# Products for the norms' sums on VectorE, a group later, and another order for the conversion of weight pieces round norms and woven groups

## What is computed

```python
for l in range(DEPTH):
    h = rmsnorm(x, norm_mix_pre[l])
    proj = h @ w_in[l]
    ...                       # three branches, gated and merged
    x = x + rmsnorm(merged @ w_o[l], norm_mix_post[l])
    h = rmsnorm(x, norm_ffn_pre[l])
    up = causal_dwconv(h @ w_up[l], ffn_conv_w[l])
    gate, val = jnp.split(up, 2, axis=-1)
    f = (jax.nn.silu(gate) * val) @ w_down[l]
    x = x + rmsnorm(f, norm_ffn_post[l])
```

## Time and profile before

| | |
|---|---|
| median of 3 runs | 1929.98 us (1924.31 to 1937.8) |
| the profiled execution | 1930.59 us |
| its span | 1928.9 us |
| TensorE busy | 1866.5 us, 97% |
| VectorE busy | 1375.6 us, 71% |
| ScalarE busy | 1083.3 us, 56% |
| GpSimd busy | 274.2 us, 14% |
| mean granted clock of TensorE | 0.986 |

### The profile page before, as it was taken

The page is one execution under the profiler, slowest core; times in us unless marked ns, Lnnn a source line. Parts: engine busy times, 40 slices in busy tenths (PEclk is TensorE's granted clock), DMA queues, the critical chain, the costliest instruction groups (busy, mean ns, idle before and its releaser), DMA issues.

```text
span 1928.9 us, 37388 instructions
## 1 busy us (share of the span) xinstructions
PE 1866.5 (97%) x15052; PEld 1818.9 (94%) x15052; DVE 1375.6 (71%) x2448; ACT 1083.3 (56%) x1820; POOL 274.2 (14%) x274
## 2 busy tenths in 40 slices
PE   7999989999999989999999999999998999999998
PEld 7999989999999989999889988999998999899998
DVE  5997678856888768876766777655557677776553
ACT  5455556654455556654666575545456757755442
POOL 1112420001103420002212103000012121030000
PEclk9999989999999989999999999999999999999999
DMA  7545535554545535564444433566544443345553
GB/s 262 170 158 187 165 121 194 182 193 142 182 159 180 167 114 199 188 207 143 153 140 137 132 131 122 177 195 195 191 161 137 148 143 117 117 164 170 192 196 111
DMA packets 86284, 315.45 MB, mean 164 GB/s; under 512 B 9568, under 2 KB 9952, under 8 KB 85984
## 3 DMA queue, kind: packets, MB, share of 16 engines
q1 hardware_dynamic: 86112, 313.06, 48.5%
HBM read 311.98 MB, written 1.05 MB: 162 GB/s over the span
## 4 chain that ended last, share of the span: by engine, by line
PE 83%; DVE 7%; ACT 6%; issue 2%; POOL 1%; DMA 0%; SPq 0%; DVEq 0%; ACTq 0%; POOLq 0%
PE big L568 73%; PE small L568 7%; ACT H L1825 3%; PE small L567 2%; DVE POOL L1305 1%; DVE L L1105 1%; DVE POOL L1189 1%; POOL POOL L2416 1%; PE small L571 0%; DVE X L1212 0%; DVE POOL L1204 0%; DVE gates L1322 0%; DVE POOL L1621 0%; DVE POOL L1434 0%; DVE POOL L1386 0%
## 5 line engine op out<-in xcount | busy, mean ns | idle before, releaser
L568 PE MATMUL big<-HH,H 128*128 128x256 f32 x3392 | 969.1, 286 | 16.8 <-DVE gates L1322 5.3
L568 PE MATMUL big<-HL,H 128*128 128x256 f32 x3392 | 948.8, 280 | 3.8 <-DVE HL L1236 3.8
L568 PE MATMUL big<-HH,L 128*128 128x256 f32 x3392 | 947.6, 279 | 0.0
L1825 ACT ACTIVATE H<-F 128x1024 fp32r<-128x1024 f32 x588 | 618.5, 1057 | 485.9 <-PE big L568 483.7
L1105 DVE TENSOR_TENSOR L<-F,H 128x1024 fp32r<-128x1024 f32 x584 | 714.7, 1232 | 197.1 <-ACT H L1825 196.6
L568 PEld LDWEIGHTS big<-HH,H 128*128 128x128 f32 x3392 | 645.0, 190 | 22.3 <-DVE gates L1322 6.0
L568 PEld LDWEIGHTS big<-HL,H 128*128 128x128 f32 x3392 | 643.1, 190 | 7.8 <-DVE HL L1236 5.2
L568 PEld LDWEIGHTS big<-HH,L 128*128 128x128 f32 x3392 | 643.3, 190 | 0.0
L568 PE MATMUL big<-FH,H 128*128 128x256 f32 x848 | 240.6, 284 | 0.1
L568 PE MATMUL big<-FL,H 128*128 128x256 f32 x848 | 236.7, 279 | 0.2
L568 PE MATMUL big<-FH,L 128*128 128x256 f32 x848 | 236.1, 278 | 0.0
(11 more groups left out here) (232 smaller groups left out, 1917.1 us busy)
## 6 DMA issues: line engine op xcount, KB each, us to landing
F<-in_stream SPq DMA_DIRECT2D x588, 512.0 KB, 3.4
X<-in_x SPq DMA_DIRECT2D x2, 512.0 KB, 4.3
out_x<-X SPq DMA_DIRECT2D x1, 1024.0 KB, 3.9
CO<-in_consts SPq DMA_DIRECT2D x1, 771.0 KB, 10.5
POOL<-in_decay SPq DMA_DIRECT2D x1, 768.0 KB, 11.8
PR<-in_params SPq DMA_DIRECT2D x1, 405.0 KB, 7.3
CO<-in_turn SPq DMA_DIRECT2D x1, 256.0 KB, 3.5
POOL<-in_lam SPq DMA_DIRECT2D x2, 128.0 KB, 3.8
```

Source lines behind the costliest of these rows:

```text
L568: return pe.e.matmul(out_, lhsT, rhs, start=start, stop=stop)
L1825: a.activation(H[:, j % NR, :], F[:, j % NF, :], ACT.Copy).then_inc(s_hi, 1)
```

## The change

1. The products x z (`xz`) of all eight j are made by VectorE in `summed`, behind the `yield`, that is in the loop turn of the next group, directly ahead of the add. The add waits for VectorE's own product instead of GpSimd's. GpSimd's `summed` is gone.
2. In ScalarE's norm the table preload stands ahead of the `HH` tiles, and for b > 0 a piece is converted behind tile 2 and another behind tile 4. Behind a group of full banks ScalarE evacuates first and converts then; the pieces of that group that begin after its middle are no longer converted in its own turn.
3. VectorE has one piece more to convert in halves ahead of and in a norm (`owed`), and two more halves in norms 1 to 4: ahead of the last normed tile and behind the last `HL` tile. Behind a group of full banks one piece is converted ahead of the evacuation of each member (`settle` with `low`).

TensorE's and SyncE's instructions stand in the same order as before.

```diff
@@ TensorE, sums_of @@
-                if j == 7:
-                    pe.wait_ge(bnd_v.sem, bnd_v.at(b, "xz"))
-                elif j:
-                    pe.wait_ge(bnd_g.sem, bnd_g.at(b, "xz", j))
+                if j:
+                    pe.wait_ge(bnd_v.sem, bnd_v.at(b, "xz", j))
@@ VectorE, norm @@
                 for n in range(KT):
+                    if n == KT - 1:
+                        low_half()
...
                     if n % 2:
                         low_x(layer, e, n - 1)
+                        if n == KT - 1:
+                            low_half()
@@ VectorE, summed @@
                 yield
-                if j == 7 and b in SUMMED:
+                if b in SUMMED:
+                    if j > 3:
+                        dve.wait_ge(bnd_v.sem, bnd_v.at(b, "add", j - 3))
                     dve.wait_ge(s_eva, m.act)
-                    v.tensor_tensor(squares_at(7, 2), X[:, j, :], tile(Z + j), ALU.mult).then_inc(
-                        bnd_v.sem, bnd_v.up(b, "xz"))
+                    v.tensor_tensor(squares_at(j, 2), X[:, j, :], tile(Z + j), ALU.mult).then_inc(
+                        bnd_v.sem, bnd_v.up(b, "xz", j))
...
-                    dve.wait_ge(bnd_g.sem, bnd_g.at(b, "xz", j))
+                    dve.wait_ge(bnd_v.sem, bnd_v.at(b, "xz", j))
@@ VectorE, settle and the main loop @@
-            def settle(n):
+            def settle(n, low=0):
                 for m in G[n].members:
+                    if low:
+                        low_parts(low)
+                        low += 1
...
                 if not made_after and full_banks(n - 1):
-                    settle(n - 1)
+                    settle(n - 1, begun_pieces(n) + AHEAD - 3)
...
                 for j in rest:
-                    low_parts(j + AHEAD)
+                    if not full_banks(n):
+                        low_parts(j + AHEAD)
                 if at_norm(n + 1):
-                    owed[0] = (G[n + 1].pos - 1) // PB + AHEAD + 1
+                    owed[0] = begun_pieces(n + 1) + AHEAD + 1
@@ ScalarE, norm @@
+                ahead = begun_pieces([n for n in range(len(G)) if fresh(n) == (True, b)][0]) + AHEAD
...
+                if e == "mix" and layer < 2:
+                    a.activation(col(1), eps, ACT.Sigmoid)
+                if e == "ffn" and layer > 1:
+                    a.activation(col(1), eps, ACT.Silu)
                 for n in range(KT):
...
                     if b == 0 and n in (1, 3, 5):
                         high_parts(2 + n // 2)
-                if e == "mix" and layer < 2:
-                    a.activation(col(1), eps, ACT.Sigmoid)
-                if e == "ffn" and layer > 1:
-                    a.activation(col(1), eps, ACT.Silu)
+                    elif b and n in (2, 4):
+                        high_parts(ahead + n // 2)
@@ ScalarE, the main loop @@
                 for j in rest:
-                    high_parts(j + 1 + AHEAD)
+                    if not full_banks(n):
+                        high_parts(j + 1 + AHEAD)
@@ GpSimd, summed: removed @@
-                q.tensor_tensor(squares_at(j, 2), X[:, j, :], tile(Z + j), ALU.mult).then_inc(
-                    bnd_g.sem, bnd_g.up(b, "xz", j))
```

More of the change, by code:

```diff
@@ L480, in norm_dve @@
                     [(b, "full", n) for n in range(KT - 1)]
-            adds = [(b, "add", j) for j in range(1, last_added(b) + 1)]
+            adds = []
+            for j in range(KT - 1):
+                adds += [(b, "xz", j)] * (b in SUMMED) + [(b, "add", j)] * (1 <= j <= last_added(b))
             if b not in SUMMED:
@@ L488, in norm_dve @@
                 rest += [(b, "x", n + 2)] * (n + 2 < KT and n % 2 == 0)
-            return adds + [(b, e) for e in ("xz", "r", "dg", "u1", "u3", "u4", "u")] + [(b, "mv", 0)] + \
+            return adds + [(b, "xz", 7)] + [(b, e) for e in ("r", "dg", "u1", "u3", "u4", "u")] + [(b, "mv", 0)] + \
                 [(b, e) for e in ("rv", "dg2")] + rest
@@ L496, in two_blocks_kernel @@
         bnd_g = tally("norm_pool", [e for b in SUMMED for e in
-                                    [(b, "xz", j) for j in range(KT - 1)] +
                                     [(b, "x", n) for n in range(1, KT, 2)]])
@@ L521, in at_norm, with begun_pieces @@
             return n < len(G) and fresh(n)[1] is not None
+        def begun_pieces(n):
+            return (G[n].pos - 1) // PB + 1
         def full_banks(n):
@@ L1370, in summed @@
                 yield
-                if j == 7 and b in SUMMED:
+                if b in SUMMED:
+                    if j > 3:
+                        dve.wait_ge(bnd_v.sem, bnd_v.at(b, "add", j - 3))
                     dve.wait_ge(s_eva, m.act)
-                    v.tensor_tensor(squares_at(7, 2), X[:, j, :], tile(Z + j), ALU.mult).then_inc(
-                        bnd_v.sem, bnd_v.up(b, "xz"))
+                    v.tensor_tensor(squares_at(j, 2), X[:, j, :], tile(Z + j), ALU.mult).then_inc(
+                        bnd_v.sem, bnd_v.up(b, "xz", j))
                 if not 1 <= j <= last_added(b):
                     return
-                n = 1
                 if b in SUMMED:
-                    n = 3
                     dve.wait_ge(bnd_a.sem, bnd_a.at(b, "zz", j))
-                    dve.wait_ge(bnd_g.sem, bnd_g.at(b, "xz", j))
+                    dve.wait_ge(bnd_v.sem, bnd_v.at(b, "xz", j))
                 else:
                     dve.wait_ge(bnd_a.sem, bnd_a.at(b, "sq", j))
-                if j > 1:
-                    dve.wait_ge(bnd_v.sem, bnd_v.at(b, "add", j - 1))
+                    if j > 1:
+                        dve.wait_ge(bnd_v.sem, bnd_v.at(b, "add", j - 1))
+                n = 3 if b in SUMMED else 1
                 v.tensor_tensor(squares_at(0, 0, n), squares_at(0, 0, n), squares_at(j, 0, n), ALU.add).then_inc(
@@ L2384, in branch_out @@
                 q.tensor_tensor(home, home, gate_tile(b, m.j), ALU.add).then_inc(mrg_g.sem, mrg_g.up(m.layer, b, m.j))
-            def summed(m):
-                b = 2 * m.layer + (1 if m.label == "out" else 2)
-                j = m.j
-                if b not in SUMMED or j == 7:
-                    return
-                gp.wait_ge(s_eva, m.act)
-                if j > 3:
-                    gp.wait_ge(bnd_v.sem, bnd_v.at(b, "add", j - 3))
-                q.tensor_tensor(squares_at(j, 2), X[:, j, :], tile(Z + j), ALU.mult).then_inc(
-                    bnd_g.sem, bnd_g.up(b, "xz", j))
             def retention(l):
@@ L2519, in settle @@
                         branch_out(m)
-                    elif m.label in ("out", "down"):
-                        summed(m)
                     elif m.label in NAMES and m.j == 3:
```

## The result

The changed kernel takes 1921.75 us (median of 20 runs, 1916.1 to 1931.74); before 1932.78 on the same chip (20 runs, 1924.31 to 1942.58). The ratio is 0.9949, 95% interval 0.993 to 0.9967: faster by half a percent, some 10 us (11.0 between the medians; the interval says 6.4 to 13.5). Forecast were 18.4 us. The profiled execution took 1917.81 (span 1916.1), 12.8 us less than the one shown of before.

A forecast was written before the change was run, and what follows sets the result against it. TensorE bounds the kernel, busy 97% of the span, so only its idle time and low-clock stretches can be won. Terms -3.3 - 5.2 - 6.9 - 3.0 = -18.4 take 1930.6 to 1912.2 us; range 1902 to 1923.

The forecast's parts named there:

- The two restarts: First groups of four, layers 0 and 1: `factor` waits go (-4.5), `fv` waits fall 1.9 to 0.7 each; -6.9 us.
- The clock behind them: After the restart waits, at 28 to 32 and 277 to 281 us, the clock would stay up: -3.0 us.
- The adds: Ahead of norms 1 and 3, products on VectorE end the adds earlier; each stall falls by 1.65, together -3.3 us.
- The term for three rounds of piece, product and add: VectorE before norm 1: 1.21 + 0.42 + 0.96 less 0.15 for overlapping starts, 2.44 us a round.
- The clock in norms 1 and 3: Shorter stalls would keep TensorE's clock higher in the small products and norms 1 and 3: 60% of 8.5, -5.2 us.
- The two conversions in ScalarE's norm, the half pieces, the table load: Work moved into gaps of ScalarE and VectorE in and around the norms; all would fit, costing 0.
- rival 5: Load doesn't fit its gap: ScalarE stands still behind it, first HH tile late in four norms, 2.4 together; 1914.6 us, chance 0.05.
- Rivals 3: Adds come no earlier: VectorE's product costs what it saves, stalls of 2.44 and the clock stay; 1920.7 us, chance 0.08.
- 1 (1920.4): Clock falls anyway: the waits shrink as worked out but every low stretch stays; 1920.4 us, chance 0.20.
- Rival 4: ScalarE's conversion after HH tile 4 blocks on a piece, HH tiles 5 to 7 come 3.7 late; 1938.1 us, chance 0.06.
- The signs of being wrong: Three wait rows still over 9 us: wrong in mechanism; under 3 with time no less than 1920: wrong in the clock.
- the three rows: TensorE's waits for VectorE's adds (4.9), ScalarE's `factor` (4.5) and its `fv` copies (3.9), 13.3 us together.

The follow-up runs named there:

- e10: The changed kernel once more, unaltered, beside e8 and e9 on one chip: 1921.32 us, ratio 0.9951.
- e7: The changed kernel with nine idle products ahead of TensorE's wait for the last add before norms 1 and 3: 1917.61 us, ratio 0.9946.
- e8: e3 with VectorE's last piece ahead of add 5 of norms 1 and 3 made behind that add: 1910.23 us, ratio 0.9895.
- e5: e3 with VectorE's product and add of a summed group made ahead of that turn's pieces: 1920.86 us, ratio 0.9958.
- e6: The changed kernel with the table preload behind the HH tiles again: one run, 1938.66 us.
- e3: The changed kernel with ScalarE evacuating before it converts behind every fg or fv group of layers 0 and 1: 1918.18 us, ratio 0.9925.
- e3b: The kernel of e3 measured a second time: 1917.7 us, ratio 0.9936.
- e9: e3 and e7 together: 1915.16 us, ratio 0.9915.

## Why the prediction was right and wrong

*The two restarts* (forecast -6.9). Right: `factor` went from 4.5 to nothing, `fv` from 3.9 to 1.3 (0.63 each, forecast 0.7), 7.1 together.

*The clock behind them* (-3.0). Right: both stretches are at 1.00 now, -3.4.

*The adds* (-3.3). The mechanism was right and the size off: the wait fell from 2.44 to 1.23 and 1.21, -2.4. The term for three rounds of piece, product and add took 2.44 each with overlapping starts. It is 2.53: an add starts 0.1 behind the end of the product that it needs, and doesn't overlap it (238.90 + 0.42 to 239.42). That is 0.27 of the 0.44 by which the stall shrank less than the 1.65 forecast; the first two adds with the product between them took 2.36 and not 2.25, which is another 0.1. GpSimd's share in the stretching was judged rightly: without it every add takes 0.96.

*The clock in norms 1 and 3* (-5.2; 60% of 8.5 is 5.1). Measured -3.4, the stretches losing 3.4 and 5.1 us and before 5.1 and 6.8, by (1 - granted clock) summed over their windows; from the 12 sums to the first HL product it is -1.6 and -1.3 (12.88 and 14.54, before 14.46 and 15.83). In e10, the same kernel, the two stretches lost 3.4 each, -5.1. So the size is right within what one profile can tell. That a shorter stall shortens them was right; e7 and e8 show that the stall had to go altogether. In the profile shown norm 2 lost 1.7 that it had not before, and in e5 3.4; in the other ten it lost nothing, so it isn't put down to the change.

*The two conversions in ScalarE's norm, the half pieces, the table load* (0). Right. The conversions fit their gaps: behind each ScalarE still waited 0.21 us for VectorE ahead of the next HH tile. The last HH tile came 0.45 later (idle 1.45 before it, 1.00 before the change), and GpSimd's last HL tile, for which 0.1 to 0.4 had been said, ended 0.7 later against the start of HH tile 6: a half piece (0.84 us, undisturbed 0.68) now runs beside GpSimd's add to `X` (1.18, before 0.73). Both were hidden. The load with its dummy ended at 11.21 in norm 0, and HH tile 0 waited on for VectorE 0.97. No drain of the kind that the Trainium skill ("ScalarE: Activation LUTs", What ACT_TABLE_LOAD costs) gives showed there either: it went as rival 5 denied. e6 adds 1 us once for the preload's place.

*The step that failed* is the sentence on parts 2 and 3, "The wait falls from 1.9 to 0.7: -1.2 at each of two places". It took the wait that ends first and didn't ask who comes late next. What ScalarE and VectorE have still to convert at the restart wasn't saved but put behind it, and the stage that follows gives them no room to catch up: 5.51 us a round against 5.44. It came back as 2.36 and 2.37 us in front of `down`, with 1.7 of clock each: +8.1. That is more than the restarts won. At 113.3 ns a product the fourth silu starts 12.36 us behind the restart in the kernel before (layer 1) and 14.62 in the changed one (both layers). Of these 2.26 us 1.3 are TensorE's earlier restart; the other microsecond is ScalarE and VectorE themselves coming later, 15.25 and not 14.28 us behind the point where TensorE stops ahead of the restart, with pieces now behind the copies and between the taps. The sum by measured terms is -2.4 - 3.4 - 7.1 - 3.4 + 8.1 + 1.7 = -6.5, near the 6.7 that the stretches show without the pace, though no exact account: its clock terms are (1 - granted clock), and small differences elsewhere are in none of its terms. Without the waits at `down` and the clock behind them, and without norm 2, the terms sum to 16.3 of the 18.4 forecast. That this much would have come is not shown: e3 and e3b, which have the change and the shorter ring, lie 14.5 and 12.3 us under before by their ratios.

*The rivals and signs.* No rival was this one. Rivals 3 (1920.7) and 1 (1920.4) came closest in time, by other mechanisms: the adds did come earlier, and the low stretches that were named did shrink. Rival 4, ScalarE blocked in the norm, did not occur. The signs of being wrong watched the three rows that were to fall, and those fell to 3.7 us, neither over 9 nor under 3; the row in which the loss stood was not among them.

*The range* held 1921.75, near its upper end. The sum was made against one profile of before and took no account of how runs of it scatter, by 1917.8 to 1950.8 us in those beside the experiments.

## What to carry to other kernels

Where a stage's engines wait for each other in a ring whose length is near TensorE's time for the same work, work that is put off at its start isn't hidden, it is handed on to the stage's end; so read, for the stage behind a removed wait, who waits for whom, and sum one round. Here a conversion put behind the evacuation that VectorE waits for shortened the ring from 5.51 to 4.76 and took the waits away. Together with one piece fewer in the row ahead of the awaited add (e8) it made the change worth about twice as much, 0.9895 against 0.9951 side by side. And before two profiles are compared as a whole, compare the time between TensorE's consecutive products stage by stage.

## What the runs showed of the hardware

- TensorE's 256-column products, with a granted clock of 1.00, follow each other every 113.3 ns or every 117.8 ns through a whole feed-forward stage (some 170 us), with the same instructions. Of 52 such stages in 13 profiles 20 ran at 117.8. One costs 6 to 7 us. The cause wasn't found: it is no wait in the profile, and no order of instructions, since of the changed kernel's own two profiles one ran none of its four stages at 117.8 and the other (e10) two. It probably makes much of the scatter of these times, but only profiled runs show it; every ratio above holds it.
- In the eight profiles where TensorE stood idle for 1.2 us ahead of the sums of norms 1 and 3, the clock fell during them (24 sums in 3.41 to 5.11 us, at full clock 2.73). With the idle time filled with idle products of 128x128 (e7, e9) or gone (e8) it stayed up through all 24 in five places of six. The low stretches at these norms lost 1.7, 3.4, 5.1 or 6.8 us each.
- With GpSimd idle VectorE's 128x768 add takes 0.96 each time; beside GpSimd's product it took up to 1.50, and the product, 0.74 alone, up to 1.63.
